# Spreading the softmax sums through a replicated tile, with the copy and the weight scaling moved in their queues

## The reference

```python
def one_block(args):                       # for each block of 128 queries
    scores = einsum('bqhd,bkhd->bhqk', q_i, k) * scale + c_i[:, :, :, None] - c[:, :, None, :]
    scores = where(causal, scores, -inf)
    probs = softmax(scores, axis=-1)
    return einsum('bhqk,bkhd->bqhd', probs, v)
m = multiscale_pool(u, w_pool, pool_scale) # trailing means, then a 128x128 product per group
mix = concatenate([rms_norm(a, g_attn_grp), rms_norm(m, g_pool_grp)], axis=-1)
h = h + rms_norm(mix @ w_out, g_mix_post)
```

## Time and profile before

| | us |
|---|---|
| median of three runs | 2226.58 |
| the profiled execution, its own time | 2228.01 |
| its span in the trace | 2226.3 |
| TensorE busy in the span | 2157.5 (97%) |
| VectorE busy | 1283.9 (58%) |
| ScalarE busy | 807.5 (36%) |
| GpSimd busy | 1038.8 (47%) |

### The profile page before, as it was taken

One profiled execution on the slowest core, in us unless ns is written; L12 is line 12 of the kernel. 1 busy time (PEld: TensorE's weight loads), 2 busy tenths in 40 slices (PEclk: granted clock), 3 DMA queues, 4 the chain that ended last, 5 costly groups with the idle time before them and its releaser, 6 DMA issues.

```text
span 2226.3 us, 31622 instructions
## 1 busy us (share of the span) xinstructions
PE 2157.5 (97%) x12220; PEld 1867.9 (84%) x12220; DVE 1283.9 (58%) x1653; ACT 807.5 (36%) x1313; POOL 1038.8 (47%) x720
## 2 busy tenths in 40 slices
PE   7999989999999999999999999999999999999898
PEld 6999977899998888888897778878888888888687
DVE  1899988810018976660004645776666656666753
ACT  3444534111227763221115764432222222222453
POOL 2788942052136656113177641055565555565600
PEclk9999999999999999999999999999999999999999
DMA  4111112311010003311302013111111111112421
GB/s 136 56 40 39 59 57 89 120 51 57 20 39 1 1 34 118 114 68 57 114 20 82 2 58 114 67 39 57 57 38 57 47 57 57 57 38 58 160 76 47
DMA packets 110603, 136.62 MB, mean 61 GB/s; under 512 B 6976, under 2 KB 92608, under 8 KB 110366
## 3 DMA queue, kind: packets, MB, share of 16 engines
q1 hardware_dynamic: 110494, 135.08, 18.6%
HBM read 118.26 MB, written 16.81 MB: 61 GB/s over the span
## 4 chain that ended last, share of the span: by engine, by line
PE 81%; DVE 9%; ACT 3%; POOL 3%; issue 3%; DMA 1%; SPq 0%; POOLq 0%; DVEq 0%; ACTq 0%
PE PS L353 48%; PE PS L2382 17%; PE PS L1724 3%; PE PS L393 2%; POOL side_sum L533 2%; PE PS L1764 2%; PE PS L1735 2%; PE PS L1777 2%; PE PS L2105 1%; DVE att L1235 1%; PE PS L382 1%; PE PS L1443 1%; DVE arg_b L1226 1%; DVE arg_a L1226 1%; DVE decay L1211 1%
## 5 line engine op out<-in xcount | busy, mean ns | idle before, releaser
L2571 DVE TENSOR_TENSOR ff_acc<-ff_acc,PS 128x512 f32<-128x512 f32 x336 | 226.8, 686 | 190.2 <-PE PS L353 189.6
L353 PE MATMUL PS<-xh,wh 128*128 128x352 f32 (+2 forms) x944 | 287.5, 336 | 5.1 <-DVE xl L448 4.0
L353 PE MATMUL PS<-xl,wh 128*128 128x352 f32 (+2 forms) x944 | 285.9, 334 | 0.0
L353 PE MATMUL PS<-xh,wl 128*128 128x352 f32 (+2 forms) x944 | 285.4, 334 | 0.0
L353 PE MATMUL PS<-wh,xh 128*128 128x256 f32 (+1 forms) x784 | 230.0, 318 | 4.4 <-DVE wl L342 3.1
L2307 POOL TENSOR_TENSOR xl<-raw,xh 128x512 fp32r<-128x512 f32 x120 | 164.5, 1379 | 139.7 <-ACT xh L2436 139.7
L353 PE MATMUL PS<-wl,xh 128*128 128x256 f32 (+1 forms) x784 | 228.8, 317 | 0.0
L353 PE MATMUL PS<-wh,xl 128*128 128x256 f32 (+1 forms) x784 | 228.3, 316 | 0.0
L576 DVE SCALAR_TENSOR_TENSOR PS<-glu,conv_vec,PS 128x1040 f32<-128x1040 f32 x184 | 225.7, 1293 | 0.8
L353 PEld LDWEIGHTS PS<-xh,wh 128*128 128x128 f32 x944 | 174.9, 188 | 13.2 <-issue 5.8
L353 PEld LDWEIGHTS PS<-xl,wh 128*128 128x128 f32 x944 | 174.4, 188 | 8.0
(11 more groups left out here) (397 smaller groups left out, 4957.1 us busy)
## 6 DMA issues: line engine op xcount, KB each, us to landing
h_rows<-rows SPq DMA_DIRECT2D x24, 512.0 KB, 2.6
rows<-h_rows SPq DMA_DIRECT2D x24, 512.0 KB, 3.4
dn_raw<-in_w_ffn_down_dram SPq DMA_DIRECT2D x22, 512.0 KB, 3.6
raw<-in_gla_w_in_dram SPq DMA_DIRECT2D x10, 1024.0 KB
raw<-in_w_ffn_gate_dram SPq DMA_DIRECT2D x20, 512.0 KB
raw<-in_w_ffn_up_dram SPq DMA_DIRECT2D x20, 512.0 KB
raw<-in_conv_w_in_dram SPq DMA_DIRECT2D x16, 512.0 KB
raw<-in_w_in_dram SPq DMA_DIRECT2D x8, 1024.0 KB
```

What stands on the lines that cost most here:

```text
L353: last = nc.tensor.matmul(out_of(c, cn), s, x[:, c0:c0 + cn], start=n == 0 and m == 0, stop=n == len(terms) - 1 and m == 2)
L2571: nc.vector.tensor_tensor(x, x, PS[:, dn_bank(p, n), :], ALU.add).then_inc(dn_left, 1)
```

## The change

A tile `sums_rep` of 128x512 is added. VectorE fills it after the reciprocals: each of the 8 values is repeated 64 times. `spread` then makes four products with 128-column weights from that tile, in place of eight with 64-column weights read from the 8 values. VectorE waits for the reciprocals to be written, and, from turn 1 on, for the spread of the turn before. ScalarE's wait ahead of the row sums of turn t is for VectorE's copy of turn t-2 in place of TensorE's spread. On ScalarE, `keep_spread` goes behind the exponentials of the pair and the second `leave`. On GpSimd, the 8 scalings of `mo_raw` go behind the masks of steps 8 to 15 in place of those of steps 11 to 18.

```diff
+        sums_rep = at("sums_rep", [P, HALF], Z0 + 32768 + 2048)
-        MASKS_AHEAD = 3
@@ pair_probs
             if h == 0 and turn > 1:
-                act.wait_ge(tail_pe, of_turn(turn - 2, SPREAD))
+                act.wait_ge(tail_dve, of_turn(turn - 2, SUMS))
@@ spread
-                for h in range(AH):
-                    out = PS[h % 2 * AD:(h % 2 + 1) * AD, 7, block_cols(h // 2)]
-                    last = nc.tensor.matmul(out, row_sums(turn)[:, h:h + 1].broadcast_to([P, AD]), ident[:], start=True, stop=True)
+                for k in range(4):
+                    last = nc.tensor.matmul(quarter(7)[:, k, :], sums_rep[:, block_cols(k)], ident[:], start=True, stop=True)
@@ attn_scalar
                     leave(2 * p - 2)
-                if turn_at(p, 1) is not None:
-                    keep_spread(turn_at(p, 1))
                 if 0 < p < PAIRS:
                     probs(2 * p)
                     probs(2 * p + 1)
@@
                 if p == PAIRS:
                     weights_high(NX - 1)
+                if turn_at(p, 1) is not None:
+                    keep_spread(turn_at(p, 1))
@@ attn_vector, sums
-                nc.vector.reciprocal(row_sums(turn), row_sums(turn)).then_inc(tail_dve, 1)
+                if turn > 0:
+                    dve.wait_ge(tail_pe, of_turn(turn - 1, SPREAD))
+                dve_own.step(dve, nc.vector.reciprocal(row_sums(turn), row_sums(turn)))
+                nc.vector.tensor_copy(sums_rep[:].rearrange("p (h d) -> p h d", h=AH),
+                                      row_sums(turn).rearrange("p (h o) -> p h o", o=1).broadcast_to([P, AH, AD])).then_inc(tail_dve, 1)
@@ attn_pool
-                k = s - AH - MASKS_AHEAD
-                if 0 <= k < KT:
-                    if k == 0:
+                if turn == 1:
+                    if h == 0:
                         pool.wait_ge(matrix_in, 16)
                         pool.wait_ge(gain_in, G6 + 64)
-                    w = mo_raw[:, k, :]
-                    nc.gpsimd.tensor_tensor(w, w, mix_gain[:, k:k + 1].broadcast_to([P, D]), ALU.mult).then_inc(pool_ready, 1)
+                    w = mo_raw[:, h, :]
+                    nc.gpsimd.tensor_tensor(w, w, mix_gain[:, h:h + 1].broadcast_to([P, D]), ALU.mult).then_inc(pool_ready, 1)
```

## The result

The changed kernel takes 2242.12 us in the median of five runs (2237.64 to 2245.97), the kernel before 2225.84 us in the median of five (2220.62 to 2228.01). The ratio, for which 17 runs with the change are on record, is 1.0077, 95% interval 1.0062 to 1.0090: slower by 14 to 20 us, where +12.9 was forecast. The profiled execution took 2243.53 us.

A forecast was written before the change was run, and what follows sets the result against it. TensorE was taken to bound the kernel; +3.5 + 1.7 + 8.6 − 1.0 + 0.1 = +12.9 us gave 2240.9 profiled, 2239.5 against the median. Its own range was 2234 to 2244, with rivals 2231 to 2247.

The forecast's parts named there:

- Term 1: Attention, pair 5: TensorE's scores wait once for step 9's reduce, whose GpSimd mask starts behind the first scaling; +3.5 us.
- Term 2: TensorE's granted clock falls behind the 3.5 us gap at pair 5; +1.7 us (bounds 0 and 1.7).
- Term 3: Turns 0 to 6: pooled's weights wait for keep_spread, now behind the second leave; +8.6 us (5 to 10).
- Term 4: TensorE's spread: four wide products hold the chain 0.89 us instead of 1.02, eight times; −1.0 us (−8 to +6).
- Term 5: VectorE's copy into the replicated tile: hidden by idle time, perhaps 0.1 late in turn 6; +0.1 us (0 to 0.6).
- rival B: Added gaps of 1 to 1.4 us make the clock fall three more times: +5.1 us, 2244.6; 15 in 100.

The follow-up runs named there:

- whole change with ScalarE's tile: The whole change, but ScalarE instead of VectorE makes the replicated tile; against the kernel before, ratio 1.0074, stage 158.09 us.
- products only: Kernel before with the four wide products and VectorE's copy into the replicated tile, ScalarE's and GpSimd's order unchanged; ratio 1.0008, stage 143.27 us.

## Why the prediction was right, and where it was not

The direction, the place and the main stalls came out. The sum was 3.4 us short of the measured +16.3 all the same. The median of 2242.12 us lies within the stated 2234 to 2244, but the room above 2239.5 had been given for the scatter of the medians and not for what fills it. By its own steps:

- **Term 1**, the scores wait for step 9's mask: +3.5 forecast, 3.3 in the kernel after, 3.5 with GpSimd's order only. Shown.
- **Term 2**, one fall of the clock behind it: 1.7 forecast and measured, in both. Shown, though its size is not fixed: in the whole change with ScalarE's tile the fall behind the same wait took 3.4.
- **Term 3**, pooled waits for keep_spread seven times: +8.6 forecast, +8.55 in the stage with ScalarE's order only, and right turn by turn (the table below). Shown.
- **Term 4**, four products for eight: −1.0 forecast, −0.7 measured, and not for the reason given. I compared two pieces of the chain; the doubled spreads show that the products cost the same and that the gain comes once a spread. The Trainium skill's "Up to 2×" for narrow tiles ("TensorEngine Tiling (Array Packing)", Theoretical Speedup) fits 16 narrow records in 0.87 us against 8 wide ones in 0.90.
- **Term 5**, VectorE's copy: +0.1 forecast (0 to 0.6), and this is the step that failed. The products only cost +2.5 in the stage, so with term 4 taken out the copy costs 3.2 us, of which TensorE's four waits are 2.9. I took its length from copies out of PSUM, 0.56 and 0.69 us, which GpSimd doesn't touch. Free, the new copy is faster than those (0.43); beside GpSimd's subtraction it lasts up to 2.25, and the idle time of VectorE that I had counted as cover (1.11 us in turn 0) shrinks with the turns, as I had said, but to less than such a copy needs.
- **Not in the sum**: a second fall of the clock, 1.7 us of full-speed work, behind the copy's longest wait in turn 6 (1322 to 1326 us). My rival B had such falls, from the gaps of term 3. Those brought none in the run that had them alone; a wait that term 5 had put at 0.1 preceded this one. That the wait caused it is not shown, as the products only had the wait without the fall.

With the measured sizes the sum is 3.5 + 1.7 + 8.6 − 0.7 + 3.2 + 1.7 = 18.0 us, against 17.1 in the stage. Where the 1 us is lost can be read from the traces. This table has the time from the start of one turn's spread (L1791, L1790 in the kernel after) to that of the next, in us; the columns behind the first are differences against the kernel before.

| from, to | before | GpSimd's order only | ScalarE's order only | products only | the three added | whole change |
|---|---|---|---|---|---|---|
| stage's start, turn 0 | 24.09 | +4.63 | 0.00 | 0.00 | +4.63 | +4.22 |
| turn 0, turn 1 | 22.55 | +0.61 | +1.49 | −0.08 | +2.02 | +2.15 |
| turn 1, turn 2 | 20.31 | −0.01 | +1.32 | −0.10 | +1.21 | +1.23 |
| turn 2, turn 3 | 17.69 | 0.00 | +1.32 | +0.23 | +1.55 | +1.55 |
| turn 3, turn 4 | 15.59 | 0.00 | +1.21 | +0.22 | +1.43 | +1.44 |
| turn 4, turn 5 | 14.52 | 0.00 | +1.22 | +0.71 | +1.93 | +1.94 |
| turn 5, turn 6 | 11.93 | 0.00 | +1.10 | +1.55 | +2.65 | +2.65 |
| turn 6, stage's end | 14.10 | +0.20 | +0.89 | −0.04 | +1.05 | +1.90 |
| stage | 140.78 | +5.43 | +8.55 | +2.49 | +16.47 | +17.08 |

From turn 1 to turn 6 the three parts add up to the whole within 0.02 us a turn, so the waits do not overlap. Around pair 5 the whole is 0.28 cheaper than its parts; TensorE's wait for the mask is 3.3 us there in place of 3.5. Behind turn 6, where the second fall stands, it is 0.85 dearer and not 1.7. So a fall that takes 1.7 us of full-speed work does not always add as much to the time: the one in turn 6 added some 0.9, the one at the stage's end 1.0, and the one behind pair 5 all of it.

On why a GpSimd instruction holds this copy and not VectorE's other work: the rows show that it does so for the copy from one SBUF tile to another. The reciprocals, from SBUF to SBUF too, keep their 0.20 us inside the subtraction (1319.28 above), and a copy from PSUM keeps its length (0.55 or 0.56 us for all of 128x384 in the stage), as in the kernel before:

```profile
1246.66 2.37 POOL L1998 TENSOR_TENSOR xl<-mix_t,xh 128x1024 fp32r<-128x1024 f32 x1
1247.11 0.56 DVE L1929 COPY prob_t<-PS 128x384 f32<-128x384 f32 x1 [0.86 <-PE PS L1764]
```

It starts inside the subtraction and ends 1.36 us before it. The Trainium skill ("SBUF — State Buffer", Who interferes with whom) states that a VectorE copy in a two-port mode and a GpSimd instruction take one shared pair of ports whole, and that the second one to start "**fully blocks** (not throttle)". The eight copies of the kernel after agree in that each ends 0.27 to 0.29 us behind a GpSimd instruction that was under way when it began. That is less than the 0.43 of a copy that meets none, so some 0.15 us of the copy must pass while it is held; no run here takes the two apart. The Trainium skill's section also says that ScalarE never waits so; ScalarE's 0.62 to 0.64 us agree. That the copy runs in a two-port mode is the Trainium skill's account, and no run here shows it. I had not weighed that rule ahead of the result.

## What to carry to other kernels

When work is moved within an engine's queue, write down what stands directly ahead of it there and which engine's last step that needs: a copy behind a leave that reads TensorE's newest transposes cost 1.2 us in each of seven turns. Before adding a VectorE copy between SBUF tiles, look at what GpSimd has under way at that moment; the copy lasted 0.4 or 2.3 us by that alone, and moving the GpSimd instruction by three steps brought it down to 0.67 and took TensorE's waits for it in those turns away. To find out whether costs add up, run the parts alone and compare them turn by turn; the total alone had left 1 us open here. A difference between two pieces of a chain is not the price of an instruction; doubling it is a cheap way to get that.

## What the runs showed of the hardware that was not expected

- VectorE's 128x512 copy from SBUF to SBUF takes 0.43 us with GpSimd idle, and ends 0.27 to 0.29 us behind the end of a GpSimd instruction that was under way, in all eight copies of the kernel after. GpSimd is held in return: its mask of 0.46 us lasts 0.64 when it starts beside the held copy.
- A narrow spread (16 records of 64-column weights) and a wide one (8 records of 128) cost TensorE 0.87 and 0.90 us at the higher clock.
- The seven gaps of 0.8 to 1.3 us on TensorE in ScalarE's order brought no fall of the granted clock; gaps of 3.3 to 3.5 us at pair 5 did in all three kernels that had one, worth 1.7 us in two of them and 3.4 in the third. A gap of 1.6 us in turn 6 was followed by a fall in two kernels and by none in a third.
- In the kernels whose stages are given, the fall at the stage's end took none, 1.7 or 3.4 us of full-speed work.
